# A residual block on one core: seven products instead of eight for inner tiles 0 to 15 of the down projection

## The reference, cut to what matters

```python
u = rms_norm(h, g_pre_ffn[i])
gate, val = jnp.split(u @ w_up[i], 2, axis=-1)
gate = causal_depthwise_conv(gate, ffn_dw_w[i], ffn_dw_b[i])
f = (jax.nn.gelu(gate, approximate=True) * val) @ w_down[i]
h = h + rms_norm(f, g_post_ffn[i])
h = h + (p[i] @ w_ple[i]) * jax.nn.sigmoid(h @ w_ple_gate[i])
```

## Time and profile before

| | |
|---|---|
| median of 3 runs | 2634.65 us (2633.25 to 2634.66) |
| the profiled execution's own time | 2633.52 us |
| its span, first to last instruction | 2631.7 us |
| matmuls | 11772 |
| first pair: up projection, down projection | about 1087 to 1512 us, 1529 to 1748 us |
| second pair: the same | about 1852 to 2277 us, 2298 to 2517 us |

### The profile page before, as it was taken

How to read it: one execution, slowest core, us unless ns; L and a number is a source line. 1 busy time by engine, 2 the same in 40 slices (tenths; PEclk the granted TensorE clock), 3 DMA queues, 4 the chain that set the end, 5 groups by cost and what they waited for, 6 DMA issues and landing times.

```text
span 2631.7 us, 32289 instructions
## 1 busy us (share of the span) xinstructions
PE 2615.2 (99%) x11772; PEld 2147.5 (82%) x11772; DVE 1606.7 (61%) x2211; ACT 808.6 (31%) x1405; POOL 1540.9 (59%) x1860
## 2 busy tenths in 40 slices
PE   9999999999999999999999999999999999999999
PEld 6888888888888888788888788888888888888887
DVE  8985879677967796767556601168745455401276
ACT  2542452444344533433232220023322222310021
POOL 6767223213321220589889853388988888743586
PEclk9999999999999999999999999999999999999999
DMA  7868787878787976354556674447444545754535
GB/s 279 312 248 323 272 321 260 291 256 317 263 288 253 320 268 237 134 173 160 184 176 219 216 296 159 152 144 276 150 149 144 169 147 170 262 194 145 172 133 176
DMA packets 275550, 579.60 MB, mean 220 GB/s; under 512 B 22976, under 2 KB 113344, under 8 KB 274752
## 3 DMA queue, kind: packets, MB, share of 16 engines
q1 hardware_dynamic: 244144, 493.64, 54.7%
q10 hardware_dynamic: 31248, 83.90, 8.3%
HBM read 422.25 MB, written 155.19 MB: 219 GB/s over the span
## 4 chain that ended last, share of the span: by engine, by line
PE 91%; DMA 3%; POOL 3%; DVE 2%; issue 1%; SPq 0%; ACT 0%; ACTq 0%; DVEq 0%
PE ps L1284 10%; PE ps L1507 10%; PE ps L1501 10%; PE ps L1503 10%; PE ps L1280 9%; PE ps L1281 9%; PE ps L1270 7%; PE ps L1272 7%; PE ps L1271 7%; PE ps L1338 2%; PE ps L1339 2%; PE ps L1342 2%; POOL w_lo L729 2%; DMA w_stage<-in_weights 2%; PE ps L1323 1%; PE ps L1320 1%
## 5 line engine op out<-in xcount | busy, mean ns | idle before, releaser
L729 POOL TENSOR_TENSOR w_lo<-w_stage,w_hi 128x256 fp32r<-128x256 f32 x1184 | 1016.9, 889 | 25.6
L725 POOL CAST w_hi<-w_stage 128x1024 fp32r<-128x1024 f32 (+2 forms) x320 | 350.6, 1096 | 532.0 <-DMA w_stage<-in_weights 346.1
L1501 PE MATMUL ps<-comb_hi,w_hi 128*128 128x512 f32 x1232 | 479.5, 389 | 1.7 <-DVE comb_lo L2045 1.4
L1503 PE MATMUL ps<-comb_lo,w_hi 128*128 128x512 f32 x1232 | 479.3, 389 | 0.0
L739 POOL TENSOR_TENSOR up_quad<-up_quad 128x128 f32<-128x128 f32 x88 | 43.9, 498 | 499.7 <-DMA up_quad<-in_up_quads 499.7
L1507 PE MATMUL ps<-comb_hi,w_lo 128*128 128x512 f32 x1232 | 330.3, 390 | 2.6 <-POOL w_lo L729 2.5
L1840 DVE SCALAR_TENSOR_TENSOR ps<-conv_in,col,ps 128x512 f32<-128x512 f32 x436 | 294.1, 747 | 0.8
L1507 PEld LDWEIGHTS ps<-comb_hi,w_lo 128*128 128x128 f32 x1232 | 230.6, 188 | 53.5 <-POOL w_lo L729 6.0
L1280 PE MATMUL ps<-ring_hi,w_hi 128*128 128x512 f32 x704 | 273.9, 389 | 0.0
L1281 PE MATMUL ps<-ring_lo,w_hi 128*128 128x512 f32 x704 | 273.9, 389 | 0.0
L1501 PEld LDWEIGHTS ps<-comb_hi,w_hi 128*128 128x128 f32 x1232 | 231.3, 188 | 50.6 <-DVE comb_lo L2045 1.9
(11 more groups left out here) (257 smaller groups left out, 4601.4 us busy)
## 6 DMA issues: line engine op xcount, KB each, us to landing
w_hi<-split_weights SPq DMA_DIRECT2D x138, 512.0 KB, 3.8
w_lo<-split_weights SPq DMA_DIRECT2D x138, 512.0 KB, 5.0
w_stage<-up_sums SPq DMA_DIRECT2D x176, 256.0 KB, 3.2
w_stage<-in_weights SPq DMA_DIRECT2D x86, 512.0 KB, 4.8
w_stage<-in_up_raw SPq DMA_DIRECT2D x132, 256.0 KB, 3.0
w_stage<-in_weights SPq DMA_DIRECT2D x64, 384.0 KB, 3.4
split_weights<-w_hi SPq DMA_DIRECT2D x46, 512.0 KB, 2.8
split_weights<-w_lo SPq DMA_DIRECT2D x46, 512.0 KB, 4.2
```

The lines of the kernel that those rows point to most:

```text
L725: nc.gpsimd.tensor_copy(w_hi[:, slot, 0:many], w_stage[:, slot, 0:many]).then_inc(w_hi_ready, 1)
L729: last = nc.gpsimd.tensor_tensor(w_lo[:, slot, k:end], w_stage[:, slot, k:end], w_hi[:, slot, k:end].bitcast(F32), ALU.subtract)
L1501: nc.tensor.matmul(ps[:, bank], w_hi[:, slot, first + k], comb_hi[i][:, k], start=start and k == 0, stop=False, skip_group_check=True)
L1503: nc.tensor.matmul(ps[:, bank], w_hi[:, slot, first + k], comb_lo[i][:, k], start=False, stop=False, skip_group_check=True)
```

## The change: what it does, and the diff

For inner tiles 0 to 15 the down projection takes 2 x 2 pieces: two inner tiles, two output tiles and the two chunks, and forms seven products in place of eight, as the up projection does. A unit `v` (eight per pair of chunks) covers four inner tiles (two such pairs, summed in PSUM) and four output tiles (two pairs `o`): 7 products x 2 x 2 inner x 3 = 84 matmuls, in 3.5 blocks of eight tiles. That is 28 blocks (`B_DN`) per pair in place of 24. Tiles 16 to 21 (`B_DL`) are done as the fourth group before.

Weights: four of seven products use sums or differences. Their sums are made by POOL with those of the up projection: 120 steps instead of 88, and `SUM_AT_BLOCK` takes in more blocks of the mixer (the first four of chunks 1 to 3, and more at the output projection). Data: each pair of inner tiles gives seven items of 128 x 512 (four raw, of which DVE overwrites some, and differences: `combine`), each rounded by ACT (`item_round`), subtracted by DVE (`item_rest`) and stored by ACT (`keep_item`), through three buffers. Tiles 16 to 21 give two items each. The last two items of an odd tile are subtracted between two of DVE's additions of the unit (`late`). The ring still has 12 places; one transfer of 1.05 MB brings an item's two parts for both inner pairs; 34 are loaded per pair, at the blocks that `RING_AT` names: two at each of the first three blocks of the per-layer projection, two at the first block of the down projection, and from its fourth block on one or two at a block in stretches. Per-layer tiles are staged in the ring's last four places before they are stored, so items 8 to 11 wait for these stores. DVE does all evictions (`add_part`): 7 x 2 per unit, copies in the first two units where nothing is there yet, else adds. ACT's copies of the first group are gone. `g_conv` has two buffers. Names of semaphores and layouts in DRAM follow.

```diff
 SUB = T // CH
 FF = 2816
 NF = FF // P
-FB = (0, 4, 10, 16, NF)
-GROUPS = len(FB) - 1
+PAIRED = 16
...
     for a in range(0, CHUNKS, 2):
         order += [(a, B_UP + i) for i in range(UPS)]
         order += [(c, B_WP + j // 4) for c, j in projected(a) if j % 4 == 0]
-        order += [(a, B_DN + i) for i in range((GROUPS - 1) * KD_)]
-        order += [(c, B_DN + (GROUPS - 1) * KD_ + j) for c in (a, a + 1) for j in range(KD_)]
+        order += [(a, B_DN + i) for i in range(DNS)]
+        order += [(c, B_DL + j) for c in (a, a + 1) for j in range(KD_)]
...
 
 SUM_PLACE = {1: 3, 2: 0, 4: 2, 5: 1}
 RAW_PLACE = {0: 0, 3: 1, 6: 3}
-SUM_STEPS = NF * H4
-SUM_AT_BLOCK = [n for n, (c, b) in enumerate(ORDER) if 1 <= c and (B_QKV <= b < B_WO or c < CHUNKS - 1 and B_WO + 4 <= b < B_WP)]
+UP_STEPS = NF * H4
+SUM_STEPS = UP_STEPS + 2 * FOURS * 4
+SUM_AT_BLOCK = [n for n, (c, b) in enumerate(ORDER) if 1 <= c and (
+    b < B_GLU + 4 or B_QKV <= b < B_WO or B_WO <= b < B_WP and (c < CHUNKS - 1 or B_WO + 4 <= b < B_WO + 7))]
 assert len(SUM_AT_BLOCK) > SUM_STEPS
...
+        def items_through(t):
+
+            if t < PAIRED:
+                return PRODUCTS * (t // 2) + (PRODUCTS if t % 2 else 2)
+            return PAIRED // 2 * PRODUCTS + 2 * (t - PAIRED + 1)
...
+        def down_bank(v, i, o):
+
+            y, xl = ((4, 0), (0, 4))[v % 2]
+            return (y, 2, y, xl, y, 2, y)[i] + o
+
+        def ring_uses(a, x):
+
+            return a // 2 * len(range(x % RING, RINGED, RING)) + x // RING + 1
+
+        RING_AT = {}
+        for held in range(RING, RINGED):
+            group, i = divmod(held - RING, PRODUCTS)
+            RING_AT.setdefault((PRODUCTS * (2 * group + 1) + i) // 2 + 3, []).append(held)
+        for held, at in zip(range(6, RING), (0, 0, 3, 4, 4, 5)):
+            RING_AT.setdefault(at, []).append(held)
...
+                step = UP_STEPS + (v % 2 * FOURS + v // 2) * 4
+                into = w_stage[:, slot, 4 * half:4 * half + 4]
+                if i in RAW_PLACE:
+                    sp.dma_start(into.rearrange("p k n -> p (k n)"), down_raw[v % 2, v // 2, RAW_PLACE[i]]).then_inc(
                         w_loaded[slot], 16)
+                else:
+                    sp.dma_start(into, sums_kept[ds(step, 4), :, ds(SUM_PLACE[i] * P, P)].rearrange(
+                        "k p n -> p k n")).then_inc(w_loaded[slot], 16)
 
...
+            def load_items(a, x):
+
+                if x < FOURS * PRODUCTS:
+                    items_stored(sp, a, items_through(x // PRODUCTS * 4 + 3))
+                else:
+                    items_stored(sp, a, items_through(PAIRED + x - FOURS * PRODUCTS))
+                if 8 <= x < RING:
+                    sp.wait_ge(ple_stored, 16 * sum(len(projected(i)) for i in range(0, a + 2, 2)))
+                sp.dma_start(ring[x % RING].bitcast(F32).rearrange("p k s t -> p (k s t)"),
+                             f_kept[x].rearrange("p k s -> p (k s)")).then_inc(ring_loaded[x % RING], 16)
...
-                    k = j if q == 0 else j - 2
-                    if 0 <= k < FB[q + 2] - FB[q + 1]:
-                        load_f(a, q + 1, k)
-                    if a == 0 and q == 1 and j < 2:
-                        sp.wait_ge(f_stored, 32 * NF)
-                        load_diff(low_b, 2, j, low_b_loaded)
-                    if a == 0 and (q, j) in ((1, 2), (2, 0)):
-                        load_raw(high_b, 3, H4, q - 1, high_b_loaded)
-                j = b - B_DN - (GROUPS - 1) * KD_
+                if 0 <= at < 3:
+                    load_items(a, 2 * at)
+                    load_items(a, 2 * at + 1)
+                if b >= B_DN:
+                    at = b - B_DN
+                    for x in RING_AT.get(at, ()):
+                        load_items(a, x)
+                    if a == 0 and 15 <= at < 17:
...
-                    act.wait_ge(f_lo_ready, unit)
-                copy(g_conv[:, :], gates[:, 2:], ACT.Identity, bias=column("ffn_b", t),
+                if t >= 2 or a:
+                    held = items_through(t - 1 if t % 2 == 0 and t <= PAIRED else t - 2) if t >= 2 else 0
+                    act.wait_ge(item_lo, a // 2 * ITEMS + held)
+                copy(g_conv[t % 2][:, :], gates[:, 2:], ACT.Identity, bias=column("ffn_b", t),
                      scale=column("ffn_w", 3 * t + 2)).then_inc(tap0_ready, 1)
 
...
+            def item_round(a, t, n):
+
+                e = a // 2 * ITEMS + items_of(t)[n]
+                if t < PAIRED and (t % 2 == 0 and n == 1 or n >= 2):
+                    act.wait_ge(f_combined, a // 2 * 2 * PAIRED + t // 2 * 4 + (1 if t % 2 == 0 else (None, None, 3, 2, 4)[n]))
+                else:
+                    act.wait_ge(ft_ready, a // 2 * NF + t + 1)
+                if e >= 3:
+                    act.wait_ge(item_stored[e % 3], 16 * (e // 3))
+                copy(item_parts[e % 3][:, 0], item_source(t, n), ACT.Copy).then_inc(item_hi, 1)
+
+            def keep_item(a, t, n):
+
+                e = a // 2 * ITEMS + items_of(t)[n]
+                act.wait_ge(item_lo, e + 1)
+                act.dma_start(item_kept(t, n), item_parts[e % 3][:, :, :].bitcast(F32).rearrange("p s t -> p (s t)")).then_inc(
+                    item_stored[e % 3], 16)
...
+                        item_round(a, t - 1, 2)
+                    for n in range(min(many, 2)):
+                        keep_item(a, t - 1, n)
                     keep_second(a, t)
-                    if t:
-                        keep_f(a, t - 1)
-                    elif a:
+                    if many > 2:
+                        keep_item(a, t - 1, 2)
...
-                act.dma_start(ple_kept[c, :, j], result(c)[:, j]).then_inc(ple_stored, 16)
+                act.dma_start(ple_kept[c, :, j], ple_stage[:, m]).then_inc(ple_stored, 16)
...
+            def down_product(a, v, i, o):
+
+                down_free(a, v, i, o)
+                at = PRODUCTS * v + i
+                b = B_DN + at // 2
+                slot, first = PLACE[a, b] % SLOTS, 4 * (at % 2) + o
+                x = v // 2 * PRODUCTS + i
+                bank = ps[:, down_bank(v, i, o)]
+                rounded_there(a, b)
+                if v % 2 == 0 and o == 0:
+                    pe.wait_ge(ring_loaded[x % RING], 16 * ring_uses(a, x))
+                parts = ring[x % RING]
+                start, stop = i in (0, 1, 3), i in (3, 5, 6)
+                for k in range(2):
+                    nc.tensor.matmul(bank, w_hi[:, slot, first + 2 * k], parts[:, k, 0], start=start and k == 0, stop=False,
+                                     skip_group_check=True)
+                    nc.tensor.matmul(bank, w_hi[:, slot, first + 2 * k], parts[:, k, 1], start=False, stop=False,
+                                     skip_group_check=True)
+                ready(a, b)
+                for k in range(2):
+                    last = nc.tensor.matmul(bank, w_lo[:, slot, first + 2 * k], parts[:, k, 0], start=False,
+                                            stop=stop and k == 1, skip_group_check=True)
+                last.then_inc(dn_tile if o == 0 else block_done if at % 2 else dn_half, 1)
...
-                        token_sums(PF, a)
-                    down_tile(a, q, j, s)
+                for v in range(2 * FOURS):
+                    for i in range(PRODUCTS):
+                        down_product(a, v, i, 0)
+                        down_product(a, v, i, 1)
+                for s in range(2):
+                    for j in range(KD_):
...
+            def combine(a, t):
+
+                even, odd = g_conv
+                before = a // 2 * 2 * PAIRED + t // 2 * 4
+                dve.wait_ge(ft_ready, a // 2 * NF + t + 1)
+                if t % 2 == 0:
+                    V.tensor_tensor(f_diff[:, :], even[:, T:], even[:, 0:T], ALU.subtract).then_inc(f_combined, 1)
+                    return
+                V.tensor_tensor(even[:, T:], odd[:, T:], even[:, T:], ALU.subtract).then_inc(f_combined, 1)
+                dve.wait_ge(f_combined, before + 1)
+                V.tensor_tensor(f_diff[:, :], odd[:, T:], f_diff[:, :], ALU.subtract).then_inc(f_combined, 1)
+                dve.wait_ge(f_combined, before + 3)
+                V.tensor_tensor(even[:, 0:T], odd[:, 0:T], f_diff[:, :], ALU.subtract).then_inc(f_combined, 1)
+
+            def item_rest(a, t, n):
+
+                e = a // 2 * ITEMS + items_of(t)[n]
+                dve.wait_ge(item_hi, e + 1)
+                V.tensor_tensor(item_parts[e % 3][:, 1], item_source(t, n), item_parts[e % 3][:, 0].bitcast(F32),
+                                ALU.subtract).then_inc(item_lo, 1)
+
...
+                    dve.wait_ge(block_done, PLACE[a, B_DN + at // 2] + 1)
+                else:
+                    dve.wait_ge(dn_half, a // 2 * DNS + at // 2 + 1)
+                j = 4 * (v % 2) + 2 * o
+                tile = (result(a)[:, j], result(a + 1)[:, j + 1], result(a + 1)[:, j], result(a)[:, j],
```

(10 more changed lines are left out.)

346 lines of the change are left out of this document (180 added, 166 removed).

## The result

The changed kernel takes 2702.74 us (median of 4 executions, 2700.87 to 2708.55) against 2634.65 us before: a ratio of 1.0263, 95% interval 1.0246 to 1.0281. It is **slower by 68 us** where 2621.5 us was forecast, and outside the range. The profiled execution took 2700.87 us with a span of 2699.0 us.

A forecast was written before the change was run, and what follows sets the result against it. PE, busy 99% of the span at 2.4 GHz, was taken as the bound. Terms -43.5 + 20 + 2 + 7 + 1.5 = -13.0 took 2633.5 to 2620.5; with 1.1 for the median, 2621.5 us, range 2598 to 2643.

The forecast's parts named there:

- Matmuls removed: Down projection, tiles 0 to 15: seven products for eight remove 192 matmuls of 0.2267 us, 43.5 us, if no gap opens.
- Small: Mixer: added sums of weights on POOL run on to the last mixer's end, 1.5 us, bounds 0 and 5; others 0.
- Up projection: Both up projections: 3 us for slowed POOL and 4 us for late copies, together 7 us, bounds 0 and 35.
- The order on ScalarE: Up projection: product 2's copy waits behind two stores, ready at 9.8 us, wanted at 10.9; 4 us charged for misses.
- Turn: From up to down projection: 3.7 MB more delays block weights; stalls of 12 and 8 us, together 20, bounds 5 and 34.
- Bursts: Inside the down projection: item loads in bursts delay block weights, 2 us for six bursts, bounds 0 and 12.
- the allowance of 7.9 us for landing: Down projection: a block's load, issued 10.9 us ahead, may take 7.9 us to land before PE waits.
- a backlog of 2.6 us: Down projection bursts: 2.62 MB per block need 6.3 us of DMA in 5.44 us, so the backlog grows to 2.6 us.
- Signs named ahead: Profile after: fuller DMA and PE waits at turns, POOL near 72% in down projection, slower POOL subtractions in up projection.
- the lock: Up projection rival: VectorE's five operations wait for POOL's subtractions, copy 1.9 us late, 30 us plus 5; total 2650, chance 0.15.
- its threshold of 1.0: Up projection: the rival decides from about 1.0 us per VectorE operation; rows showed 0.80 on average, 0.88 in one run.

The follow-up runs named there:

- e_swap: Changed kernel with SyncE issuing each sums step's quad load before the store of the last step's sums: 2673.10 us, ratio 1.0152, mixer 1082.7 us.

## Why the prediction was wrong, step by step

- **Matmuls removed, -43.5: right.** In stretches without stalls they start 0.2267 us apart, and each down projection has 96 fewer.
- **Small, +1.5 with an upper bound of 5: wrong, it took +27.8, the farthest outside its bounds.** The step that failed is "sums of weights go to POOL while it has nothing else". POOL did have time. I counted the engine and not the queue: each step puts a load, POOL's sums and a store in a chain on SP, in front of the next block's weights. With the load issued ahead of the store the same steps cost nothing (e_swap).
- **Up projection, +7: +35.7, just past its bounds of 0 to 35, and in us the largest error.** The order on ScalarE was named and sized: copy needed 10.9 us into the unit, expected at 9.8. It ended at 12.7 (2125.62 - 2112.92); the tile itself was done 0.7 us later than I had it (5.5 against 4.8). The term that was mis-sized is the duration of a 512-column operation: 0.80 us was half of one of 1024 columns, and a wait that comes once for an operation does not halve with it. It measured 1.10 to 1.40. The first pair had other places that I did not cost, ScalarE's first copy and the mixer's work ahead of the value add.
- **Turn, +20 with 12 and 8: about +28.** Step and first 72 matmuls together gave 6.3 + 10.2 = 16.5 and 2.0 + 9.2 = 11.2 us. The mechanism was right and so was its size: the stalls proper, at the last projection block and the first two down blocks, are 12.0 and 8.3 us. The rest is mostly a price that I had left out, PE at half its clock behind a stall (below): 20 and 11 matmuls, 4.0 and 2.2 us.
- **Bursts, +2 with an upper bound of 12: +19.9.** The step that failed is the allowance of 7.9 us for landing against a backlog of 2.6 us. I counted weights and items, and not what SP loads there in the first pair for the next up projection (`low_b` and `high_b`, lines 618 and 613). The second pair has none and still lost 8.0 us; that a late block delays the next one's load, so that the backlog does not drain, is my reading of it, and was not tried by itself.
- **Signs named ahead.** "If PE loses over 20 us there, the lock was right": it lost 35.7 in the up projection, and in the second pair the gaps stand before the fifth product of even units, as named. POOL's subtraction was to rise from 901 to 980 ns and took 950. In the down projection its rows above show 2.79 us for four, so adds that read PSUM did not slow them; POOL was busy there for 68% (72% was forecast). The DMA engines were full for 40 us around each turn, not longer than before.
- **The lock as a rival, 0.15:** its mechanism ran, at 1.24 us an operation (6.2 / 5) above its threshold of 1.0, and priced the up projection at 35 us. That this meets the 35.7 is in part luck: 30 of its 35 were for the copy of product 2, for which PE waited 17.9 us in 18 stalls; much of the rest stood at places that the rival did not have. Its total of 2650 fell short by the mixer and the bursts, and by 8 us at the turn.

## What to carry to other kernels

Before adding work to an idle engine, follow the queue that feeds it: a store that waits for that engine, in front of a load that others wait for, makes the idle engine's latency everybody's. Where a tuned schedule is near its limit, take an operation's price from one of its own size and surroundings, not as a fraction of a larger one. And a change that saves on the bounding engine may be lost in orders that cost nothing to mend: here swapping two issues was worth 28 us, and spreading the loads some 30 by the stages.
